# Reordering the head groups of two attention layers, and moving the rotation of the index key from GpSimd to VectorE

## The reference, cut to what matters

```python
proj = h @ w_in[l]                       # 3656 columns
(mq, mk, mv, dq, dk, dv, sq, sk, sv, iq, ik, iw) = jnp.split(proj, offsets, axis=-1)
moba = moba_attention(qk(mq), qk(mk), mv)        # main: 4 heads of 64, causal at 256 positions
diff = diff_attention(...)                        # difference: 4 heads, (softmax1 - lam * softmax2) @ v, v 128 wide
diff = rms_norm(diff, diff_subln_g[l]) * (1.0 - lam_init)
# sparse: index score = sum_h iw_h * relu(iq_h . ik); the top 64 keys of each query
dsa = dsa_attention(qk(sq), qk(sk), sv, rope(iq), rope(ik), iw * (IDX_HEADS ** -0.5))
x = x + concat(moba, diff, dsa) @ w_out[l]
x = x + (silu(h2 @ w_gate[l]) * (h2 @ w_up[l])) @ w_down[l]    # h2: normed x
```

## Time and profile before

| | |
|---|---|
| median of 3 runs | 1314.15 us (1314.12 to 1315.04) |
| profiled execution, its own time | 1313.64 us |
| its span | 1311.8 us |
| TensorE busy | 1265.5 us, 96% |
| VectorE, ScalarE, GpSimd busy | 821.8, 664.2, 196.6 us |
| mean granted clock of TensorE | 0.979 |

### The profile page before, as it was taken

The page is one execution under the profiler, slowest core; times in us unless marked ns, Lnnn a source line. Parts: engine busy times, 40 slices in busy tenths (PEclk is TensorE's granted clock), DMA queues, the critical chain, the costliest instruction groups (busy, mean ns, idle before and its releaser), DMA issues.

```text
span 1311.8 us, 16910 instructions
## 1 busy us (share of the span) xinstructions
PE 1265.5 (96%) x6430; PEld 1067.9 (81%) x6430; DVE 821.8 (63%) x975; ACT 664.2 (51%) x981; POOL 196.6 (15%) x186
## 2 busy tenths in 40 slices
PE   8997999999999979999999999999999999999998
PEld 6776888888887868888888899788998777788886
DVE  6897365555569945555556765776686677744454
ACT  5566354444465644544445454565455744544443
POOL 5884100000276711000000000000000003000000
PEclk9999799999999969999999998999999999999999
DMA  7344046555462332555555463423324455455551
GB/s 256 141 152 166 33 152 216 183 189 207 152 215 87 127 129 97 212 182 185 189 188 200 149 247 137 161 79 142 129 97 175 146 193 184 169 208 190 181 201 51
DMA packets 34218, 213.11 MB, mean 162 GB/s; under 512 B 4305, under 2 KB 5585, under 8 KB 11506
## 3 DMA queue, kind: packets, MB, share of 16 engines
q1 hardware_dynamic: 34098, 212.21, 45.4%
q0 software_dynamic: 64, 0.13, 0.0%
HBM read 211.28 MB, written 1.05 MB: 162 GB/s over the span
## 4 chain that ended last, share of the span: by engine, by line
PE 73%; DVE 13%; issue 4%; POOL 4%; ACT 4%; DMA 2%; SPq 0%; POOLq 0%; DVEq 0%; ACTq 0%
PE bank L598 20%; PE bank L600 20%; PE bank L599 20%; DVE wlo L1689 4%; PE bank L1007 3%; PE bank L764 2%; PE bank L705 2%; DVE index L1769 2%; ACT whi L1233 1%; PE bank L724 1%; PE bank L852 1%; PE bank L626 1%; DMA raw<-in_w_out 1%; ACT probs L1310 1%; DVE index L1788 1%
## 5 line engine op out<-in xcount | busy, mean ns | idle before, releaser
L1689 DVE TENSOR_TENSOR wlo<-raw,whi 128x2048 fp32r<-128x2048 f32 (+3 forms) x197 | 444.3, 2262 | 253.7 <-ACT whi L1233 252.7
L1233 ACT ACTIVATE whi<-raw 128x2048 fp32r<-128x2048 f32 (+5 forms) x201 | 369.2, 1843 | 160.7 <-PE bank L600 149.7
L598 PE MATMUL bank<-whi,hT_hi 128*128 128x512 f32 (+4 forms) x1040 | 406.5, 391 | 8.8 <-DVE wlo L1689 5.2
L600 PE MATMUL bank<-whi,hT_lo 128*128 128x512 f32 (+4 forms) x1040 | 398.4, 383 | 0.0
L599 PE MATMUL bank<-wlo,hT_hi 128*128 128x512 f32 (+4 forms) x1040 | 397.8, 383 | 0.0
L598 PEld LDWEIGHTS bank<-whi,hT_hi 128*128 128x128 f32 x1040 | 196.6, 189 | 48.0 <-DVE wlo L1689 8.9
L600 PEld LDWEIGHTS bank<-whi,hT_lo 128*128 128x128 f32 x1040 | 196.4, 189 | 36.4
L599 PEld LDWEIGHTS bank<-wlo,hT_hi 128*128 128x128 f32 x1040 | 196.8, 189 | 33.1
L598 PE MATMUL bank<-whi,mixT_hi 128*128 128x512 f32 (+1 forms) x248 | 96.1, 387 | 3.7 <-DVE mixT_lo L1724 1.6
L600 PE MATMUL bank<-whi,mixT_lo 128*128 128x512 f32 (+1 forms) x248 | 93.7, 378 | 0.0
L598 PE MATMUL bank<-whi,ffT_hi 128*128 128x512 f32 x240 | 93.7, 390 | 0.0
(11 more groups left out here) (282 smaller groups left out, 1532.2 us busy)
## 6 DMA issues: line engine op xcount, KB each, us to landing
raw<-in_ff_loop SPq DMA_DIRECT2D x90, 1024.0 KB, 4.8
raw<-in_w_groups SPq DMA_DIRECT2D x64, 1024.0 KB, 4.8
raw<-in_w_out SPq DMA_DIRECT2D x8, 1024.0 KB, 5.4
raw<-in_ff_first SPq DMA_DIRECT2D x6, 1024.0 KB, 4.9
raw<-in_w_values SPq DMA_DIRECT2D x8, 728.0 KB, 4.1
raw<-in_w_comp SPq DMA_DIRECT2D x4, 1024.0 KB, 6.4
raw<-in_ff_last SPq DMA_DIRECT2D x3, 1024.0 KB, 6.7
raw<-in_w_values SPq DMA_DIRECT2D x4, 736.0 KB, 6.6
```

What stands on the lines that cost most here:

```text
L598: eng.matmul(out, lhsT=hi, rhs=wh, start=start, stop=False)
L600: return eng.matmul(out, lhsT=lo, rhs=wh, start=False, stop=stop)
L1233: eng.activation(whi[j][:, 0:n], raw[j][:, 0:n], ACT.Copy).then_inc(hi_ready, 1)
L1689: eng.tensor_tensor(wlo[j][:, 0:n], raw[j][:, 0:n], whi[j][:, 0:n].bitcast(F32), ALU.subtract).then_inc(lo_ready, 1)
```

## The change

The groups run in the order main, difference, sparse, difference, and the head sets in the order main, difference query, difference key, sparse. The columns of the weights, of `z` and of `mix`, and the rows of the output weights follow. All three value and index products are of 368, 364 and 364 columns as before, but the last two input products are now both value products (6 and 7), and the parts of the last stand around the scores of the sparse group. Each engine's list is written anew. The index key is rotated by VectorE (`index_key`, four instructions, result in `sqr`) and signals `key_ready`; the scale of the index weights moves into the ReLU. `prep` counts five sets a layer where it counted six. The first output product waits for the copies of the last group, which is now a difference group; the mix halves are turned after the sparse values and after the first three output parts.

```diff
-IQ, DQ, DK, MQ, MK, SQ, SK, IK, IW, DV, MV, SV = (
-    0, 512, 1024, 1536, 1792, 2048, 2304, 2560, 2624, 2632, 3144, 3400)
-PRODUCTS = ((IQ, 512), (IK, 368), (DQ, 512), (DK, 512), (MQ, 512), (IK + 368, 364), (SQ, 512), (IK + 732, 364))
-HEAD_PRODUCTS = (2, 3, 4, 6)
-VALUE_PRODUCTS = (1, 5, 7)
-HEAD_SETS = (DQ, DK, MQ, SQ)
+IQ, DQ, DK, MQ, MK, SQ, SK, IK, IW, VALUES = 0, 512, 1024, 1536, 1792, 2048, 2304, 2560, 2624, 2632
+PRODUCTS = ((IQ, 512), (IK, 368), (MQ, 512), (DQ, 512), (DK, 512), (SQ, 512), (IK + 368, 364), (IK + 732, 364))
+VALUE_PRODUCTS = (1, 6, 7)
+HEAD_SETS = (MQ, DQ, DK, SQ)
+HEAD_PRODUCTS = (2, 3, 4, 5)
+HEAD_GAINS = ((0, 3), (1,), (4,), (2, 5))
...
+TURNED_SETS = ((T_IQ, IQ), (T_IK, None), (T_MQ, MQ), (T_DQ, DQ), (T_DK, DK), (T_SQ, SQ))
 CHUNKS1 = 54
+GROUPS = ((T_MQ, T_MK, 2, 1), (T_DQ, T_DK, 4, 6), (T_SQ, T_SK, 5, 7), (T_DQ + 2, T_DK + 2, 4, 7))
+DIFF_GROUPS = (1, 3)
...
-                eng.wait_ge(prep, l * 6 + 1)
-                for r in range(RT):
-                    projected(1, r)
-                    src = z[:, r, IK:IK + HD].rearrange("p (n d) -> p n d", d=HD)
-                    rotate(src, [rope_c[:, r, :]], [rope_s[:, r, :]], 1)
-                    pool(eng.tensor_scalar(z[:, r, IW:IW + IDX_HEADS], z[:, r, IW:IW + IDX_HEADS],
-                                           IDX_HEADS ** -0.5, None, ALU.mult))
-                pool.wait(eng)
-                for r in range(RT):
-                    ins = eng.tensor_copy(scr_ik(r).rearrange("p (a d) -> p a d", a=2),
-                                          z[:, r, IK:IK + HD].unsqueeze(1).to_broadcast([P, 2, HD]))
-                    if r:
-                        ins.then_inc(prep, 1)
-                    else:
-                        pool(ins)
-
-                for s, (c0, p, gains) in enumerate(zip(HEAD_SETS, HEAD_PRODUCTS, ((1,), (4,), (0, 3), (2, 5)))):
-                    eng.wait_ge(prep, l * 6 + 2 + s)
+                for s, (c0, p, gains) in enumerate(zip(HEAD_SETS, HEAD_PRODUCTS, HEAD_GAINS)):
+                    eng.wait_ge(prep, l * 5 + 1 + s)
...
-                        eng.wait_ge(pT_act, 2 * A + 8 + r + 1)
+                        eng.wait_ge(pT_act, 2 * A + 10)
+                        eng.wait_ge(pT_dve, A + 5)
...
+                    if s == 1:
+                        eng.wait_ge(key_ready, l + 1)
+                    else:
+                        eng.wait_ge(prep, l * 5 + s + (s == 0))
...
+                    c0 = VALUES + g * SEQ
+                    for r in range(RT):
+                        eng.wait_ge(z_rows[r], l * 8 + GROUPS[g][3] + 1)
...
+                row_product(2, 0, 0); row_product(2, 0, 1); turn_heads(0, 0); turn_heads(0, 1)
+                row_product(2, 1, 0); turn_heads(1, 0); row_product(2, 1, 1); index_scores(l, 0)
+                index_scores(l, 1); row_product(3, 0, 0); row_product(3, 0, 1); row_product(3, 1, 0)
+                row_product(3, 1, 1); row_product(4, 0, 0); index_scores(l, 2); index_scores(l, 3)
+                index_scores(l, 4); turn_heads(2, 0); index_scores(l, 5); turn_heads(2, 1); row_product(4, 0, 1)
+                group_scores(0); row_product(4, 1, 0); row_product(4, 1, 1); row_product(5, 0, 0)
+                row_product(5, 0, 1); row_product(5, 1, 0); turn_heads(3, 0); group_turn(0); turn_heads(3, 1)
+                row_product(5, 1, 1); group_values(0); turn_heads(4, 0); turn_heads(4, 1); row_product(6, 0, 0)
+                group_scores(1); row_product(6, 0, 1); row_product(6, 1, 0); row_product(6, 1, 1)
+                row_product(7, 0, 0); group_turn(1); turn_heads(5, 0); turn_heads(5, 1); row_product(7, 0, 1)
+                group_scores(2); row_product(7, 1, 0); row_product(7, 1, 1); group_values(1); group_turn(2)
+                group_scores(3); group_values(2); mix_turn(0, 0); mix_turn(0, 1); group_turn(3)
+                out_product(0, 0, 0); group_values(3); out_product(0, 0, 1); out_product(1, 0, 0)
+                mix_turn(1, 0); mix_turn(1, 1); out_product(1, 0, 1); out_product(0, 1, 0); out_product(0, 1, 1)
...
-                eng.activation(probs[:, u % 3, :], bank[2 + u % 3][:, :], ACT.Relu, scale=HD ** -0.5)\
+                eng.activation(probs[:, u % 3, :], bank[2 + u % 3][:, :], ACT.Relu, scale=(HD * IDX_HEADS) ** -0.5)\
...
+                copy_z(l, 1, 0); copy_z(l, 1, 1); hi(3, 0); hi(3, 1); heads_copy(l, 0, 0); heads_copy(l, 0, 1)
+                copy_z(l, 2, 0); square_heads(l, 0, 0); heads_copy(l, 1, 0); hi(4, 0); index_relu(l, 0)
+                index_relu(l, 1); copy_z(l, 2, 1); square_heads(l, 0, 1); hi(4, 1); scale_heads(l, 0)
+                copy_z(l, 3, 0); square_heads(l, 1, 0); hi(5, 0); copy_z(l, 3, 1); square_heads(l, 1, 1)
+                index_relu(l, 2); index_relu(l, 3); index_relu(l, 4); heads_copy(l, 2, 0); index_relu(l, 5)
+                heads_copy(l, 2, 1); hi(5, 1); scale_heads(l, 1); copy_z(l, 4, 0); square_heads(l, 2, 0)
+                hi(6, 0); copy_z(l, 4, 1); square_heads(l, 2, 1); attend_exp(A + 0, 0, (0, 1)); hi(6, 1)
+                scale_heads(l, 2); attend_exp(A + 0, 0, (2,)); heads_copy(l, 3, 0); copy_z(l, 5, 0)
+                attend_copy(A + 0, 0); square_heads(l, 3, 0); attend_copy(A + 0, 1); heads_copy(l, 3, 1)
+                hi(7, 0); copy_z(l, 5, 1); square_heads(l, 3, 1); heads_copy(l, 4, 0); heads_copy(l, 4, 1)
+                scale_heads(l, 3); attend_exp(A + 1, 1); copy_z(l, 6, 0); copy_z(l, 6, 1); hi(7, 1)
+                split_hi(t0, 17); heads_copy(l, 5, 0); blend_copy(A + 1); heads_copy(l, 5, 1); split_hi(t0, 18)
+                attend_exp(A + 2, 0, in_bank=False); copy_z(l, 7, 0); split_hi(t0, 19); attend_copy(A + 2, 0)
+                attend_copy(A + 2, 1); diff_stats(l, 1); copy_z(l, 7, 1); attend_exp(A + 3, 1)
+                turned_hi_copy(l * 3 + 1, mixT, halves=(0,)); blend_copy(A + 3); diff_stats(l, 3)
...
+            def index_key(l):
+
+                for r in range(RT):
+                    eng.wait_ge(z_rows[r], l * 8 + VALUE_PRODUCTS[0] + 1)
+                h, key = HD // 2, z[:, :, IK:IK + HD]
+                dve(eng.tensor_tensor(turned_key[:, :, 0:h], key[:, :, h:HD], rope_s[:, :, 0:h], ALU.mult))
+                dve(eng.tensor_tensor(turned_key[:, :, h:HD], key[:, :, 0:h], rope_s[:, :, h:HD], ALU.mult))
+                dve.wait(eng)
+                dve(eng.tensor_tensor(key, key, rope_c[:, :, :], ALU.mult))
+                dve.wait(eng)
+                eng.tensor_tensor(sqr[:, 0:2 * P].rearrange("p (r a d) -> p r a d", r=RT, a=2),
+                                  key.unsqueeze(2).to_broadcast([P, RT, 2, HD]), turned_key[:, :, :].unsqueeze(2).to_broadcast([P, RT, 2, HD]),
+                                  ALU.add).then_inc(key_ready, 1)
...
+                lo(1, 0); lo(1, 1); lambda_sums(l); lo(2, 0); lo(2, 1); lambda_value(l); index_key(l); lo(3, 0)
+                lo(3, 1); head_sums(l, 0, 0); lo(4, 0); index_sum(l, 0); index_sum(l, 1); head_sums(l, 0, 1)
+                lo(4, 1); head_sums(l, 1, 0); lo(5, 0); index_sum(l, 2); index_sum(l, 3); index_sum(l, 4)
+                index_sum(l, 5); head_sums(l, 1, 1); topk_rounds(0, 1); lo(5, 1); topk_rounds(1, 3)
+                head_sums(l, 2, 0); attend_mask(A + 0, causal); head_sums(l, 2, 1); lo(6, 0); topk_rounds(3, 4)
+                lo(6, 1); attend_copy(A + 0); topk_rounds(4, 8); topk_mask(); attend_out(A + 0, 0, take(0))
+                head_sums(l, 3, 0); head_sums(l, 3, 1); attend_mask(A + 1, causal); lo(7, 0); blend(A + 1, 1)
+                lo(7, 1); blend_copy(A + 1); split_lo(t0, 17); attend_mask(A + 2, chosen); attend_copy(A + 2)
+                lo_from_pool(2 * l + 1); split_lo(t0, 19); diff_norm(l, 1); mixed(1); attend_mask(A + 3, causal)
+                attend_out(A + 2, 0, take(2)); blend(A + 3, 1); turned_lo_copy(l * 3 + 1, mixT, halves=(0,))
+                blend_copy(A + 3); diff_norm(l, 3); mixed(3); turned_lo_copy(l * 3 + 1, mixT, halves=(1,))
+                lo_from_pool(2 * l + 2); split_lo(t0, FFN1); add_out(0, 0); add_out(0, 1)
...
+    values = np.concatenate([ik, iw, mv, dv[:, :, :SEQ], sv, dv[:, :, SEQ:]], 2)
...
+    m_rows, d0_rows, d1_rows, s_rows = np.split(i["w_out"], 4, axis=1)
+    t["w1_out"] = np.stack([halves(g) for g in np.concatenate([m_rows, d0_rows, s_rows, d1_rows], 1)])
```

More of the change, by code:

```diff
@@ L205, in block_one_and_two @@
         heads_copied = [sem(f"heads_copied{b}") for b in range(2)]
+        key_ready = sem("key_ready")
         idx_ready = sem("idx_ready")
@@ L405, in _ @@
                     else:
-                        src = t["w1_groups"][l, HEAD_PRODUCTS.index(p) + 1]
+                        src = t["w1_groups"][l, PRODUCTS[p][0] // COLS]
                     for j in range(2):
@@ L944, in group_turn @@
                 def group_turn(g):
-                    if g < 2:
-                        blend_turn(A + g, 2 * l + g)
+                    if g in DIFF_GROUPS:
+                        blend_turn(A + g, 2 * l + DIFF_GROUPS.index(g))
```

(21 more changed lines are left out.)

64 lines of the change are left out of this document (14 added, 50 removed).

## The result

The kernel after the change takes **1301.99 us** (median of 4 runs, 1301.40 to 1303.37) against 1314.13 before in the same job: ratio 0.9909, interval 0.9892 to 0.9926. That is 12.1 us faster, inside the range, and about half of the forecast gain of 22.3. The profiled execution took 1302.03 us, its span 1300.2, 11.6 less than before.

What follows compares the result with a forecast made beforehand. TensorE, busy 96%, was taken as the bound. Layer 0: 17.7 - 6.1 - 0.4 = 11.2; layer 1: 18.8 - 6.1 - 1.6 = 11.1; together 22.3 off 1313.64 gives 1291.3, stated as 1291 us, range 1281 to 1304.

Steps and rivals of the forecast that it cites:

- The mechanism: Sparse group's softmax: two 364-column product parts (about 4 us) between its scores and transposes remove the 4.67 us wait.
- The tail: After the last input product: new TensorE waits of 1.5, 1.0, 2.6, 0.9 and 0.1, sum 6.1 us a layer.
- the rival of the falling clock: Tail of each attention: TensorE's clock falls all the same during a handful of transposes; 1297 or 1311; chance 0.2.
- its cheap case: Tail: dense work from +15.5 lifts the fallen clock 5.5 us later, costing 2.8 us a layer, 1297.
- the stretch before the tail: Input products before the tail: no gain expected; idle 4.05 us a layer, net -0.4 and -1.6; bounds 0 to 8.
- The 1.8 us placed at the main group's transposes: Before the tail: short TensorE wait because the main group's mask stands behind top-k rounds; part of 3.7 us.
- The sum: Both layers: gains of 11.2 and 11.1, together 22.3 us, giving 1291.3 us.
- The middle: Rival, before the tail: VectorE or GpSimd bounds, head sets three and four late; 8 not 3.7 a layer, 1300; chance 0.16.
- those of being right: Sparse exponential waits at most 1 us, three to four 1-3 us gaps, clock near 1.00, no key wait, tails 11 us shorter.
- those of being wrong: Earlier waits on GpSimd head sets or low halves; clock 0.5 after last blend; output-weight load ahead of ScalarE's conversion.
- The key: Index key on VectorE: four instructions taken at 2 us, bounds 1.2 to 4, covered before TensorE needs the low halves.
- Slower: Rival, ScalarE's in-order queue: last head set from GpSimd late, everything slides; at 15 us late 1322; chance 0.03.

Runs made afterwards that it cites:

- the filled tail: Kernel after the change with 5, 4 and 10 unused matmuls before the last scores, sparse values and last group's transposes: 0.9869, 1297.89 us.
- Undone in two ways: Kernel after the change, main set's turns moved behind the next product part: 0.9857; or GpSimd rotating both rows before waiting for scales: 0.9851.
- Alone in the old order: Kernel before, with only the index key moved to VectorE and the weights' scale in the ReLU: 0.9991, 1313.41 us.
- a kernel slower: Rotation first, early mask and filled tail waits (0.9821), plus the main group's last exponentials tile moved earlier in ScalarE's list: 0.9865, 1297.59 us.

## Why the prediction came out about half right

- **The mechanism holds.** Two product parts over the sparse group's softmax took the wait of 4.67 and 5.20 us away, and the key's with it.
- **The tail** was to put back 6.1 us a layer in waits of 1.5, 1.0, 2.6, 0.9 and 0.1 at full clock. Measured are 1.10, 0.89 and 0.84, together 2.83, and of the 10.2 us at half clock 9.4 are no wait and count 4.7: together 7.5 in either layer. The two parts belong together. The fall comes between the second wait and the third, and there VectorE's blend sets the time, not TensorE:

```profile
135.57 0.69 PE L720 MATMUL bank<-ident,probs 128*128 128x128 f32 x2 [0.84 <-DVE probs L1865]
```

```profile
134.16 0.58 PE L724 MATMUL bank<-ident,probs 128*128 128x128 f32 x2 [2.62 <-DVE probs L1869]
```

The first is the kernel after, the second the one with both rows rotated first, whose clock was full up to here. Both stand 9.6 us behind the start of the last scores (126.01 and 124.59). So at full clock the waits are 1.1, 0.9 and 2.6, 4.6 in place of 6.1 (the last two small ones were not seen in this kernel), and what the fall costs is the 5.6 us at half clock behind the third wait, 2.8. That is the price of the rival of the falling clock in its cheap case (2.8 a layer, 1297), and the filled tail confirms it: 5.3 us by the ratios for 2 x 2.8. The argument against that rival, that gaps of 1.0 to 1.2 us had left the clock full, was the weak point.
- **The step that failed** is the stretch before the tail, "0.35 at the turn of the index query ... and 3.7 in short waits", net -0.4 and -1.6. Measured: idle 4.23 and 3.37, and of the 6.8 us at half clock 6.4 and 6.5 are no part of the wait and cost 3.2 in each layer: 7.4 and 6.6 in place of 4.05. The cause is the main set, for whose turn the prediction placed no wait. From the head scale to the end GpSimd needs 10.5 us, because row 1's rotation stands behind the wait for the scale and because of two collisions with VectorE. Undone in two ways, this gave 6.8 and 7.6 us by the ratios (0.9857 and 0.9851 against 0.9909), with intervals apart from that of the kernel after. Which share the collisions have by themselves no run shows. The 1.8 us placed at the main group's transposes exists (2.4 to 2.6), but only once the wait ahead of it is gone; the kernel has them in a row and pays the first.
- **The sum.** 1291.3 + (7.4 - 4.05) + (6.6 - 4.05) + 1.4 + 1.4 = 1300.0. The stretch behind layer 1's attention took 1.8 more than before: 1301.8, against 1302.0 measured. The traces place that too. In the third block, whose instructions the change leaves alone, the clock is at half for 6.8 us before and for 10.2 after, 1.7 us more; the first row is the kernel before:

```profile
803.00:811.00 8.00, 8.00 (x38) 7.96 (x38) 3.49 (x10) 1.99 (x2) 0.00 (x0) 0.57 0.00 1
```

```profile
789.00:800.00 11.00, 11.00 (x54) 10.96 (x54) 4.09 (x12) 2.59 (x3) 0.00 (x0) 0.53 0.00 0
```

It differs so between the other kernels as well; what sets it off is open.
- **Two rivals came true at once**, each in part. The middle was priced at 2 x 4.3 = 8.6 us over the forecast and cost 5.9. Its mechanism was half right: VectorE's two-input work collides with GpSimd's and TensorE waits at a turn, but it is the first head set that is late, not the third and fourth, and not through the key. The clock was priced at 5.6 and cost that, less the 1.5 a layer by which the tail's waits came out smaller: about 2.8 in all. Both at full price would have given 1305, outside the range; that the time lies inside it owes something to luck.
- **The signs.** Of those of being right, no wait for exponentials and none for the key came; the clock of the tails did not stay near 1.00 (0.90 in the windows above), and the two attentions together with the stretch before became 6.3 and 6.5 us shorter, not 11 each. Of those of being wrong, two came: a wait on a head set from GpSimd, and half clock behind the last blend.
- **The key** was taken at 2 us and took 3.0 (0.47, 0.78, 1.38, 0.42), within its bounds, and no wait followed in this order. Alone in the old order it moved its own gain into the wait for a low half.
- **Slower** did not come near: the last head set was turned without a wait.

## What to carry to other kernels

Where several waits stand in a row on the engine that bounds, the profile shows only the first at its full size: undo it and read the next before counting the gain. Ask what an in-order engine could do while it waits: GpSimd stood 7.47 us with the next row's rotation still to do, and rotating both rows first was worth about as much as moving TensorE's turn. Price a gap by what it does to the clock too: gaps of 1 us among small matmuls set off 10.2 us at half clock a layer, and unneeded matmuls in them gave 5 us back. Count of it only what lies where TensorE bounds: 2.8 of 4.7 us here. And taking one wait away made a kernel slower where the next grew from 0.55 to 2.3. Last, look at a stretch that the change leaves alone: here it varied by 5 us between traces, more than several of the gains compared.
